# Gain vectors applied behind the transpose, a reordered start and a later tap transpose in a 256-token, four-layer fp32 kernel

## What is computed

```python
def rmsnorm(x, g):
    y = xf * lax.rsqrt(jnp.mean(xf * xf, axis=-1, keepdims=True) + NORM_EPS)
    return y * g
for i in range(2):                       # first block
    hn = rmsnorm(h, norm_g[i])
    q, k, v, z = split(hn @ w_in)        # then rope, and attention (i=0 sliding window with sinks, i=1 causal)
    h = h + (o * silu(z)) @ w_out[i]
h = rmsnorm(h, final_g)
for layer in range(2):                   # second block
    h = h + hybrid_mixer(rmsnorm(h, norm_mix[layer]), ...)   # dilated attention and a state-space scan
    h = h + (silu(hn2 @ w_gate) * (hn2 @ w_up)) @ w_down     # hn2 = rmsnorm(h, norm_ffn[layer])
return rmsnorm(h, final_norm)
```

## Time and profile before

| | us |
|---|---|
| three executions | 948.77, 948.79, 952.5 |
| median | 948.79 |
| span of the profiled execution | 950.1 |
| TensorE busy | 916.7 (96%) |
| VectorE busy | 570.3 (60%) |
| ScalarE busy | 517.6 (54%) |

### The profile page before, as it was taken

The page is one execution under the profiler, slowest core; times in us unless marked ns, Lnnn a source line. Parts: engine busy times, 40 slices in busy tenths (PEclk is TensorE's granted clock), DMA queues, the critical chain, the costliest instruction groups (busy, mean ns, idle before and its releaser), DMA issues.

```text
span 950.1 us, 12341 instructions
## 1 busy us (share of the span) xinstructions
PE 916.7 (96%) x4605; PEld 743.3 (78%) x4605; DVE 570.3 (60%) x921; ACT 517.6 (54%) x853; POOL 127.4 (13%) x103
## 2 busy tenths in 40 slices
PE   5899998999999999999999999999999999999996
PEld 4777877777887788888888888877888788888884
DVE  4744487644877567785555544765676865555443
ACT  4456646565475787564444433566676554444331
POOL 0031013302104343000000000023340000000000
PEclk9899999999999999999999999999999999999998
DMA  9531243532444332466555555452332665555531
GB/s 312 189 128 59 90 163 102 167 130 89 136 157 136 130 133 89 137 220 219 177 181 191 197 186 180 160 172 90 133 126 97 221 203 193 181 177 179 192 117 44
DMA packets 94845, 146.87 MB, mean 155 GB/s; under 512 B 6476, under 2 KB 54852, under 8 KB 94788
## 3 DMA queue, kind: packets, MB, share of 16 engines
q1 hardware_dynamic: 91392, 139.14, 43.5%
q0 software_dynamic: 1440, 5.24, 1.8%
q10 hardware_dynamic: 1956, 1.71, 0.5%
HBM read 145.04 MB, written 1.05 MB: 154 GB/s over the span
## 4 chain that ended last, share of the span: by engine, by line
PE 68%; issue 21%; DVE 6%; ACT 2%; DMA 2%; POOL 0%; ACTq 0%; POOLq 0%; DVEq 0%
PE bank L999 51%; PE bank L974 6%; PE bank L1051 2%; PE bank L1050 2%; PE bank L1071 2%; PE bank L1137 1%; DVE lo L900 1%; PE bank L1073 1%; PE bank L1072 1%; DMA taps_stage<-in_conv_b 1%; ACT junk L1182 1%; PE bank L1047 1%; DMA gains<-in_norm_g 1%; ACT hi L1157 1%; DVE hyb_MT L1745 1%
## 5 line engine op out<-in xcount | busy, mean ns | idle before, releaser
L900 DVE TENSOR_TENSOR lo<-raw,hi 128x1024 fp32r<-128x1024 f32 x246 | 300.6, 1247 | 140.9 <-ACT hi L1157 138.5
L1157 ACT ACTIVATE hi<-raw 128x1024 fp32r<-128x1024 f32 x262 | 268.6, 1057 | 75.9 <-PE bank L999 68.8
L999 PE MATMUL bank<-hi,xT_hi 128*128 128x512 f32 (+2 forms) x736 | 294.7, 400 | 8.5 <-DVE lo L900 3.1
L999 PE MATMUL bank<-hi,xT_lo 128*128 128x512 f32 (+2 forms) x736 | 285.4, 388 | 0.0
L999 PE MATMUL bank<-lo,xT_hi 128*128 128x512 f32 (+2 forms) x736 | 284.6, 387 | 0.0
L999 PEld LDWEIGHTS bank<-hi,xT_hi 128*128 128x128 f32 x736 | 140.1, 190 | 37.5 <-issue 9.8
L999 PEld LDWEIGHTS bank<-hi,xT_lo 128*128 128x128 f32 x736 | 139.6, 190 | 29.0
L999 PEld LDWEIGHTS bank<-lo,xT_hi 128*128 128x128 f32 x736 | 140.3, 191 | 25.4 <-issue 0.5
L999 PE MATMUL bank<-hi,hT 128*128 128x512 f32 x352 | 111.5, 396 | 0.0
L999 PEld LDWEIGHTS bank<-hi,hT 128*128 128x128 f32 x352 | 66.1, 188 | 15.4
L999 PE MATMUL bank<-lo,hT 128*128 128x512 f32 x176 | 69.4, 394 | 0.0
(11 more groups left out here) (233 smaller groups left out, 1057.6 us busy)
## 6 DMA issues: line engine op xcount, KB each, us to landing
raw<-in_w_in SPq DMA_DIRECT2D x26, 1024.0 KB, 4.9
raw<-in_w_gate SPq DMA_DIRECT2D x44, 512.0 KB, 3.7
raw<-in_w_up SPq DMA_DIRECT2D x44, 512.0 KB, 4.6
raw<-in_w_down SPq DMA_DIRECT2D x22, 1024.0 KB, 4.8
raw<-in_w_out SPq DMA_DIRECT2D x20, 1024.0 KB, 5.0
raw<-in_w_in_b SPq DMA_DIRECT2D x10, 1024.0 KB, 5.0
raw<-in_w_in_a SPq DMA_DIRECT2D x8, 1024.0 KB, 7.4
gains<-in_norm_g POOLq DMA_DIRECT2D x2, 512.0 KB, 6.1
```

The source lines that it names most:

```text
L900: return engine.tensor_tensor(lo[r][:, cols], raw[c.i % RAW][:, cols], hi[r][:, cols].bitcast(F32), ALU.subtract)
L999: last = nc.tensor.matmul(bank[:, 0:wd], still[a], mv[r][:, off:off + wd], start=c.first and i == 0 and j == 0, stop=c.last and i == len(t ...
L1157: nc.scalar.activation(hi[c.i % SPLIT][:, cols], raw[c.i % RAW][:, cols], ACT.Copy)\
```

## The change

1. Gain vectors are no longer multiplied into h before the transpose. The raw h is transposed (step `xturn`, TensorE), VectorE multiplies the PSUM bank with a column of gains while writing `quarter`, ScalarE copies `quarter` to `xT_hi` and VectorE subtracts (step `xsplit`). The 56 columns `gcol` are made once: four small DMAs on ScalarE's queue, one transpose, a copy and a product. The repeated `gains` rows are loaded only for the group norms and the last norm; the product of two gain rows (`mid_gain`) goes.
2. The first weight chunk comes in four DMAs, and is split in four pieces.
3. TensorE does 8 matmuls on a tile of ones before the first transposes and 6 behind them.
4. The taps' transpose moves to the second mixer.

```diff
 def turn_x(sc, n, *ms):
+    turns = []
     for m in ms or range(M):
-        sc.turned[n, m] = sc.turn(sc.filled[n, m], "x", 4 * n, m)
+        b = sc.bank()
+        s = sc.step("xturn", n=n, m=m, bank=b, gain=sc.gain_now, buf=sc.count.get("xturn", 0) % 2,
+                    added=sc.added.get((n, m)))
+        b.freed = (s, "vector")
+        turns.append(s)
+    for s in turns:
+        sc.turned[n, s.m] = sc.step("xsplit", of=s, n=n, m=s.m)
...
                 if n == 0:
                     add(sc, bs[0], 0, 0)
-                    times_gain(sc, 0, 0)
                 else:
                     turn_x(sc, 0, 0)
                     add(sc, bs[1], 1, 0)
-                    times_gain(sc, 1, 0)
...
-    if sc.heads == 16:
+    if sc.heads == 32:
...
-                    for half in range(2):
-                        dst = slot[:, half_of(c, half)].rearrange("p (k n) -> p k n", n=cw)
-                        n = len(ks) // 2
-                        sp.dma_start(dst, wt[:, n * half:n * (half + 1), c0:c0 + cw]).then_inc(raw_in[0] if half else raw_first, 16)
+                    for k in ks:
+                        sp.dma_start(slot[:, k * cw:(k + 1) * cw], wt[:, k, c0:c0 + cw])\
+                          .then_inc(raw_first[k] if k < 3 else raw_in[0], 16)
...
+        def warmed(n):
+
+            for _ in range(n):
+                nc.tensor.matmul(psum[7][:, :], warm[:, 0:P], warm[:, :], start=True, stop=True)
+
+        pe.wait_ge(warm_up, 1)
+        warmed(8)
         pe.wait_ge(const_in, 16)
         for s in sc.steps:
+            if s.kind == "begin":
+                warmed(6)
...
+            elif s.kind == "xturn":
+                if s.added is not None:
+                    ended(pe, s.added, "vector")
+                else:
+                    pe.wait_ge(x_in if s.n else x_first[s.m], 16)
+                bank = freed(pe, s.bank)
+                for i in range(4):
+                    c0 = s.n * 512 + i * P
+                    last = transpose(bank[:, i * P:(i + 1) * P], h[:, s.m, c0:c0 + P])
+                last.then_inc(sem["xturn", "tensor"], 1)
...
+            elif s.kind == "xsplit":
+                ended(act, s.of, "vector")
+                done(nc.scalar.activation(xT[0][:, 4 * s.n:4 * s.n + 4, s.m * P:(s.m + 1) * P],
+                                          quarter[s.of.buf][:, :].rearrange("p (k t) -> p k t", k=4), ACT.Copy), s)
...
-        load_gain(sc.gains[0])
...
+            elif s.kind == "xturn":
+                dve.wait_ge(sem["xturn", "tensor"], s.i + 1)
+                g = gcol[:, s.gain + 4 * s.n:s.gain + 4 * s.n + 4]
+                done(tt(quarter[s.buf][:, :].rearrange("p (k t) -> p k t", k=4),
+                        psum[4 + s.bank.at][:, :].rearrange("p (k t) -> p k t", k=4),
+                        spread(g.unsqueeze(2), [P, 4, P]), ALU.mult), s)
+            elif s.kind == "xsplit":
+                ended(dve, s, "scalar")
+                a, b = (x[:, 4 * s.n:4 * s.n + 4, s.m * P:(s.m + 1) * P] for x in xT)
+                done(tt(b, quarter[s.of.buf][:, :].rearrange("p (k t) -> p k t", k=4), a.bitcast(F32), ALU.subtract), s)
```

More of the change, by code:

```diff
@@ L63 @@
 M_SCAN, M_SEL = 3 * QC, 3 * QC + P
+G_A, G_MIX, G_FFN, G_FIRST = 0, 16, 32, 48
 def constants():
@@ L205, in gain @@
     def gain(self, src):
-        if src is not None:
-            self.loaded += 1
-        g = {"src": src, "i": len(self.gains), "loaded": self.loaded, "users": [], "made": None}
+        self.loaded += 1
+        g = {"src": src, "i": len(self.gains), "loaded": self.loaded, "users": []}
         self.gains.append(g)
@@ L579, in next_gain @@
     def next_gain():
-        sc.gain_now = sc.gain(("norm_ffn", layer))
+        sc.gain_now = G_FFN + KD * layer
     out_product(sc, w["out"], 12, {
@@ L603, in hybrid @@
         b["evac"] = [pend, pend]
-    sc.gain_now = sc.gain(last_gain)
+    if layer == 0:
+        sc.gain_now = G_MIX + KD
+    else:
+        last = sc.gain(("final", 0))
     b0, b1 = sc.block(512), sc.block(512)
@@ L624, in hybrid @@
         add(sc, b1, 1, 1)
-        for m in range(M):
-            times_gain(sc, 1, m)
         norm_goes_on(sc, False)
@@ L630, in hybrid @@
         for m in range(M):
-            scaled = sc.step("scaled", n=0, m=m, gain=sc.gain_now)
+            scaled = sc.step("scaled", n=0, m=m, gain=last)
         for m in range(M):
@@ L674 @@
 PARTS = {
-    "chunk": ("tensor", "scalar", "vector", "gpsimd"), "gained": ("vector",), "turn": ("tensor", "scalar", "vector"),
-    "taps": ("tensor", "scalar"), "mid_gain": ("vector",), "square": ("scalar",), "meansq": ("vector", "gpsimd"), "newton": ("vector",), "added": ("vector",),
+    "chunk": ("tensor", "scalar", "vector", "gpsimd"), "columns": ("tensor", "vector"), "xturn": ("tensor", "vector"),
+    "xsplit": ("scalar", "vector"), "turn": ("tensor", "scalar", "vector"),
+    "taps": ("tensor", "scalar"), "square": ("scalar",), "meansq": ("vector", "gpsimd"), "newton": ("vector",), "added": ("vector",),
     "ev_kv": ("scalar",), "ev_q": ("scalar",), "ev_z": ("scalar",), "ev_x": ("scalar",),
@@ L981, in _ @@
                     ended(pe, x, "vector")
-                if half == 0:
+                if half == 0 and c.i:
                     split_done(pe, c.i, 0)
@@ L1149, in split @@
             if c.i == 0:
-                act.wait_ge(raw_in[0] if half else raw_first, 16)
-            elif half == 0:
+                cw = c.size // 4
+                for k in (2 * half, 2 * half + 1):
+                    act.wait_ge(raw_first[k] if k < 3 else raw_in[0], 16)
+                    cols = slice(k * cw, (k + 1) * cw)
+                    nc.scalar.activation(hi[0][:, cols], raw[0][:, cols], ACT.Copy)\
+                      .then_inc(sem["chunk", "scalar"] if k % 2 else first_hi, 1)
+                return
+            if half == 0:
                 act.wait_ge(raw_in[c.i % RAW], arrived[c.i])
@@ L1384, in _ @@
         pool.wait_ge(chain["gpsimd"], links["gpsimd"])
-        after = {id(sc.gains[g["i"] - 1]["users"][-1]): g for g in sc.gains[1:] if g["src"] is not None}
+        after = {id(sc.gains[g["i"] - 1]["users"][-1]): g for g in sc.gains[1:]}
         for s in sc.steps:
@@ L1389, in _ @@
             if s.kind in ("chunk", "rest"):
+                if s.kind == "rest" and s.i == SETUP_AT:
+                    load_gain(sc.gains[0])
                 for i, half in due(s):
@@ L1459, in split @@
         def split(c, half):
+            if c.i == 0:
+                cw = c.size // 4
+                for k in (2 * half, 2 * half + 1):
+                    dve.wait_ge(*((sem["chunk", "scalar"], half + 1) if k % 2 else (first_hi, half + 1)))
+                    cols = slice(k * cw, (k + 1) * cw)
+                    tt(lo[0][:, cols], raw[0][:, cols], hi[0][:, cols].bitcast(F32), ALU.subtract)\
+                        .then_inc(sem["chunk", "vector"] if k % 2 else first_lo, 1)
+                return
             dve.wait_ge(sem["chunk", "scalar"], 2 * c.i + half + 1)
@@ L1533, in tables @@
             chained(ts(small[:, :, 1, :], small[:, :, 1, :], -1.0, None, ALU.mult))
+        nc.vector.memset(warm[:, :], 1.0).then_inc(warm_up, 1)
         for s in sc.steps:
```

115 lines of the change are left out of this document (55 added, 60 removed).

## The result

The changed kernel takes **962.8 us** (median of 4 executions, 962.48 to 964.68), the kernel before 950.6 in the same set (948.77 to 952.85): ratio 1.0125, 95% interval 1.010 to 1.0149. That is slower, as forecast. It lies only 0.2 us inside the outer range (945.5 to 963) and above the forecast's own (953.5 to 960); the 957.0 us were 5.8 too low. The profiled executions differ by 1.1 us less than the medians (12.1): the span is 961.0 us instead of 950.1, and the last matmul ends at 952.15 instead of 941.13, **+11.0** where the sum said +8.25.

What follows compares the result with a forecast made beforehand. TensorE, busy 916.7 of 950.1 us, was taken as the bound, through its waits. Terms -7.5 + 4.8 + 3.65 + 3.4 + 1.6 + 2.3 = +8.25 on 948.79 gave 957.0 us, own range 953.5 to 960, outer 945.5 to 963.

Steps and rivals of the forecast that it cites:

- outer range: Whole kernel: 945.5 to 963 us, leaving out most of the case of no loss at the later norms.
- The start: Up to the keys' transpose: earlier first product, no taps' wait, VectorE then limiting; -7.5 us, bounds -5.8 and -9.
- VectorE's slack swallows it: Start: whether matmuls on ones warm the clock changes little, as VectorE has 5.8 us of slack before the keys' transpose.
- part 1: The start of the kernel, up to the keys' transpose, forecast as one sum of -7.5 us.
- The later norms: VectorE's serial line delays TensorE: FFNs +2.4 each, second mixer +3.65, first hybrid layer +3.4, second hybrid layer +2.3.
- VectorE's idle time before `xT_lo`: All 24 turns: rises from 8.9 us to about 24 times 0.6, 15 us.
- clock term: Before the first hybrid layer alone: the wait growing to 4.8 us loses TensorE's clock, +1.6 us, upper end 2.5.
- The boundaries are hidden: Rival, later norms: products overlap copies or earlier transposes absorb the delay, +0 there, 941.3 us; chance 0.17.
- half of it: Rival, later norms: gaps of 1 to 2 us, no clock loss, some +7, 948 us, no change; chance 0.13.
- The clock falls at each new gap: Rival, before both FFNs: clock lost at 2.1 us gaps, +1.6 to 2.5 each, 960 to 962 us; chance 0.15.
- The start gives less: Rival, start: small gain loads land as late as `gains` did, -5.8, 958.7 us; within the forecast's 0.55 chance.
- The page's rule: Norm turns: extra VectorE cycles from PSUM and ScalarE cycles from SBUF, 1 us at most over 24 turns, 958 us.

Runs made afterwards that it cites:

- ninth experiment: The changed kernel run once more with no edit; 961.8 us, ratio 1.0115.
- fifth experiment: The changed kernel without its 14 matmuls on ones; 963.2 us, ratio 1.0125.
- tenth: The kernel before with only the taps' transpose moved to the second mixer; 946.3 us, ratio 0.995.
- sixth experiment: The changed kernel with the taps' transpose back in the first mixer; 966.5 us, ratio 1.0162.
- third experiment: The changed kernel with VectorE's product issued ahead of the weight split where a turn comes right behind that split; 948.6 us, ratio 0.9964.
- second: The kernel before, its start kept, with gain columns behind the transpose at the five later norms; 968.8 us, ratio 1.0177.
- fourth: The changed kernel with the norm before the first hybrid layer put back to a gain row ahead of the transpose; 957.7 us, ratio 1.0069.
- eleventh: The changed kernel with products ahead of splits and gain rows at the norms before both hybrid layers; 944.2 us, ratio 0.9923.
- twelfth experiment: The eighth experiment with the taps' two loads issued by SyncE behind later chunks' weights instead of by ScalarE; 942.7 us, ratio 0.991.
- first: The changed kernel with its new start kept and gain rows ahead of the transpose at the five later norms; 945.2 us, ratio 0.9936.
- seventh: The changed kernel with its first weights in two pieces, split in halves, instead of four; 964.8 us, ratio 1.0122.
- eighth experiment: The changed kernel with rows at the five later norms and the first norm's second-half products ahead of chunk 1's splits; 943.4 us, ratio 0.9919.

## Why the prediction was right, and where it was short

The mechanism was right and the size too small: the measured time is inside the outer range by 0.2 us only, which is luck. The median of the ninth experiment, the same kernel, is 1.0 us lower.

**The start: right** (-7.5 against -7.2; first product at 10.06 against "near 10.5", `xT_lo` of (1, 0) at 18.75 against 18.8, keys' transpose at 41.52 against 41.5). "Whether the ones warm the clock changes little: VectorE's slack swallows it" holds by the fifth experiment. What it consists of is shown now: 4.8 us are the taps' transpose alone (tenth), and the same transpose put back costs 5.3 at the keys' transpose (sixth). The prediction gave part 1 as one sum and did not ask what the taps' transpose was worth by itself.

**The later norms: right, term by term.** The replay of VectorE's line gave +2.4, +2.4, +3.65, +3.4 and +2.3, measured +2.35, +2.3, +3.7, +3.2 and +2.35. That it is the order, and not columns, copies from SBUF or the place of the transposes, was only argued there; the third experiment shows it for most of the loss, where the order alone takes back 14 us of the median and 13.5 in the traces, 11.6 of them at the later norms. Of the 5 us that stay at the later norms, 3.1 are before the hybrid layers and 2.0 in the second mixer; whether another order would take those too isn't shown. The forecast that VectorE's idle time before `xT_lo` would rise to 15 us was too high (12.9): it took the whole copy at each of 24 turns, but where two turns follow each other, as at 16.71 to 18.57, the second product runs beside the first copy.

**What failed is the clock term.** The step was "TensorE's 1.6 us wait becomes 4.8. That is longer than the 2.8 that lost the clock, so I add what the slow matmuls cost there, 7.03 - 5.46 = 1.6", with nothing added anywhere else. It measured 2.4 there (granted clock 0.57 over 271 to 279 us). In the second mixer, where the wait grew from 2.8 to 4.0, 24 matmuls took 8.08 us instead of 7.03, +1.05. And the gate's wait, unchanged at 2.02 us, cost 1.55. Together that is 3.4 more than forecast; with the 0.7 made good at 308 us and the small errors of the other terms it makes the 2.7 between +8.25 and +11.0. The gate's part differs from one execution to the next (ninth experiment), so it is no cost of the change, but of the one execution that was profiled; the other two come with the longer waits.

**The time it was added to was low too.** The forecast went from 948.79, the median of three executions, while the sum was read from a slower execution. The prediction took that one to be the one of 952.5 us, 2.4 above its span. In every execution that is listed with its span the time is 1.75 to 1.95 us above it, so the profiled one took about 952.0 and is none of the three. In the set with the result the kernel before has 950.6, and 950.7 to 952.3 in the others. That is 1.9 of the 5.8 us; 2.7 come from the terms above; and the last 1.1 are there because the profiled execution of the kernel before was some 1.3 us slower than its median and that of the changed kernel was not, so that the last matmuls of the two profiles lie less far apart (11.0) than the medians (12.1).

**The rivals.** *The boundaries are hidden* and *half of it* fell with the waits. *The clock falls at each new gap* has the time nearest to the measured one (960 to 962) with the wrong places: at the FFNs, which it named, the clock stayed full in both executions of the changed kernel. *The start gives less* fell: the small loads landed by 5.3 us (in the fifth experiment TensorE waits 5.3 for the last of them).

**The page's rule.** ScalarE's copy takes 631 ns from SBUF, where the same copy from PSUM took 597 ns in the mean of its 24 (0.60 us in the earlier trace rows). VectorE's product takes 685 ns from PSUM, 690 from SBUF; its subtraction 692 with both operands in SBUF, 689 with one in PSUM (groups L1608 and L1614 above). By the Trainium skill, page "VectorE: DVE Perf Modes", section "The TRN2 errata — SBUF-src ops pay a fixed extra latency per instruction", ScalarE pays 52 cycles more from SBUF, 0.043 us as the prediction worked out: the trace agrees in sign and nearly in size. The same table's 62 cycles more for VectorE from PSUM do not show in these rows. Neither moves the sum by much: 24 times 0.034 is 0.8 us at most.

## What to carry to other kernels

Where one engine does A, another B on A's result, and the first then C on B's, the first stands idle for B's length unless something lies between A and C in its list; look for the independent operation that is already there (here the weight split, 1.22 us against a copy of 0.63) and put it between, and A as early as its input allows. Here that was worth 14 us of 963. Removing rows and loads from the start brought nothing that could be measured beside moving the one operation that waited for a late DMA: before taking a start apart, ask of each wait whether the waiting operation is needed there at all. For changes of half a per cent count with the price of the clock at every wait that is lengthened, and take the base from many executions, not from the one with the profile.

## What the runs showed of the hardware

Whether a wait of about 2 us costs TensorE's clock is not settled by its length or place in the program. The same wait of 2.02 us for the gate left the clock at 2.4 GHz in the profiled executions of the kernel before and of the second, fourth, fifth, sixth, ninth, eleventh and twelfth experiment, and at 1.2 GHz behind it in the changed kernel and the first, third, seventh, eighth and tenth; waits of 1.84 to 1.89 before the FFNs kept it in both executions of the changed kernel and in the sixth experiment, and lost it at one of two in the second, fourth, fifth and seventh. The same 1.84 to 1.89 before the second mixer never lost it, in seven executions. The wait of 2.7 to 2.8 us in the second mixer lost it in the kernel before, the eighth and the twelfth experiment and kept it in the first and the tenth. A loss behind a wait of 2 us costs 1.4 to 1.7 us. The waits of 2.9 to 4.5 us lost it in every execution that was profiled. The mean granted clock tells it for executions without a trace: of 16 executions of the kernel before in one set, the three at 0.997 took 948.0 to 948.6 us, the three at 0.990 with the longest times 955.0 to 955.3. The difference of 0.007 over 950 us is 6.7 us of full clock, about the difference of the times. So its own spread is 0.8%, over half of what this change does.

At the start it is the same. The 14 matmuls on ones warmed the clock for the first products in the execution of the result (12 matmuls 0.23 us apart), and in the ninth experiment, the same kernel, it was half there (0.66 over 10 to 15 us). The Trainium skill, page "TensorE: Matmul & The Clock Gate", section "Part 1: The HAM clock gate", says that the number of slow matmuls at a kernel's start varies from run to run of the same kernel; the trace agrees, and here it is true of short waits in the middle of the kernel too.

The issue of a load can hold the issuing engine's own work: behind the two loads of the taps, 48 and 12 KB, ScalarE's list stood still for 3.77 and 2.29 us in the eighth experiment (0.45 and 3.90 in the changed kernel), while the issues ahead of them took about 0.5 each. It is not a matter of these two alone: in the first experiment 3.08 us fell on a load of 16 KB, the fourth from the end of the same row of issues (`small<-in_d_skip`), and the taps' loads took 1.63 and 1.12. The last four issues of the row together took 4.1 to 7.1 us in the profiled executions that have the two. Without the two (twelfth), two of the others still took 1.30 and 0.91. Whether the number of the issues or their shape counts wasn't tried.
